# A hybrid diffusion backbone on one core: expert outputs of units 0 to 4 written as gated rows to DRAM, and another order of vector work at the dense mixer's start

## The reference

```python
def swiglu(x, wg, wu, wd):
    return (jax.nn.silu(x @ wg) * (x @ wu)) @ wd      # hidden width 2816

def moe_swiglu(x, w_router, wg, wu, wd):
    xt = x.reshape(-1, d)                              # 256 tokens
    logits = (xt @ w_router).astype(jnp.float32)
    top_v, top_i = lax.top_k(logits, TOP_K)            # 2 of 8
    top_w = jax.nn.softmax(top_v, axis=-1)
    gate = jnp.sum(jax.nn.one_hot(top_i, N_EXPERTS) * top_w[..., None], axis=1)
    out = jnp.zeros_like(xt)
    for e in range(N_EXPERTS):
        out = out + gate[:, e:e + 1] * swiglu(xt, wg[e], wu[e], wd[e])
    return out.reshape(bsz, t_len, d)
```

## Time and profile before

| | us |
|---|---|
| median of three runs (1506.99 to 1511.18) | 1510.18 |
| the profiled execution | 1505.23 |
| its span, from first to last instruction | 1503.3 |
| TensorE busy in it | 1446.7 (96%) |
| VectorE / ScalarE busy | 539.9 / 305.0 |

### The profile page before, as it was taken

The page is one execution under the profiler, slowest core; times in us unless marked ns, Lnnn a source line. Parts: engine busy times, 40 slices in busy tenths (PEclk is TensorE's granted clock), DMA queues, the critical chain, the costliest instruction groups (busy, mean ns, idle before and its releaser), DMA issues.

```text
span 1503.3 us, 60959 instructions
## 1 busy us (share of the span) xinstructions
PE 1446.7 (96%) x27189; PEld 1279.1 (85%) x27189; DVE 539.9 (36%) x1480; ACT 305.0 (20%) x877; POOL 26.0 (2%) x48
## 2 busy tenths in 40 slices
PE   5999998999999999999999999999999999999997
PEld 3888587999547787888878989999999999999996
DVE  1474426666637354888722210010101010010102
ACT  2112423000103523455342010100101010010101
POOL 0100000000000000100000000000000000000000
PEclk9999999999999999999999999999999999999999
DMA  9823849444449132100155999999999999999995
GB/s 390 320 94 123 312 162 408 173 170 167 177 168 350 56 127 86 36 8 6 35 228 200 419 378 408 417 380 418 376 419 382 413 418 372 418 381 418 381 411 227
DMA packets 71418, 406.98 MB, mean 271 GB/s; under 512 B 8530, under 2 KB 8964, under 8 KB 34436
## 3 DMA queue, kind: packets, MB, share of 16 engines
q1 hardware_dynamic: 68752, 399.96, 67.2%
q0 software_dynamic: 1440, 2.89, 0.7%
q10 hardware_dynamic: 1108, 2.41, 0.4%
HBM read 403.31 MB, written 1.92 MB: 270 GB/s over the span
## 4 chain that ended last, share of the span: by engine, by line
PE 92%; DVE 3%; DMA 2%; ACT 2%; issue 1%; ACTq 0%; DVEq 0%
PE banks L1648 28%; PE banks L1668 14%; PE banks L1030 9%; PE banks L1067 4%; PE banks L678 3%; PE banks L681 3%; PE banks L784 3%; PE banks L787 3%; PE banks L1194 2%; PE banks L1253 2%; PE banks L1630 2%; PE banks L1614 1%; PE banks L1271 1%; PE banks L704 1%; PE banks L820 1%; PE banks L1282 1%
## 5 line engine op out<-in xcount | busy, mean ns | idle before, releaser
L1648 PE MATMUL banks<-w,ring 128*64 128x86 f32 x11264 | 455.6, 237 | 1.4 <-issue 0.9
L1648 PEld LDWEIGHTS banks<-w,ring 128*64 128x64 f32 x11264 | 435.5, 136 | 9.9 <-issue 9.1
L1668 PE MATMUL banks<-w,ring 128*64 128x86 f32 x5632 | 242.1, 238 | 0.0
L3134 DVE TENSOR_TENSOR w<-w,banks 128x86 f32<-128x86 f32 x176 | 43.1, 245 | 551.7 <-PE banks L1648 544.0
L1668 PEld LDWEIGHTS banks<-w,ring 128*64 128x64 f32 x5632 | 224.1, 137 | 0.2 <-issue 0.2
L2193 ACT ACTIVATE w<-banks 128x86 f32<-128x86 f32 x176 | 42.7, 243 | 573.2 <-PE banks L1648 573.2
L704 PE MATMUL banks<-ring,ct 128*32 128x256 f32 x768 | 47.6, 396 | 2.3 <-ACT ct L1759 2.1
L678 PE MATMUL banks<-w,ring 128*128 128x256 f32 x224 | 49.2, 380 | 0.6 <-issue 0.3
L681 PE MATMUL banks<-ring,w 128*128 128x256 f32 x224 | 48.9, 379 | 0.0
L678 PEld LDWEIGHTS banks<-w,ring 128*128 128x128 f32 x224 | 42.3, 190 | 7.4 <-issue 1.8
L1030 PE MATMUL banks<-ht,ring 128*128 128x128 f32 x352 | 44.6, 282 | 3.0 <-DVE ht L2262 3.0
(11 more groups left out here) (466 smaller groups left out, 1757.6 us busy)
## 6 DMA issues: line engine op xcount, KB each, us to landing
ring<-in_moe_gu SPq DMA_DIRECT2D x176, 1024.0 KB, 8.7
ring<-in_moe_w_down SPq DMA_DIRECT2D x176, 512.0 KB, 8.8
ring<-in_ada_w SPq DMA_DIRECT2D x48, 1024.0 KB, 5.1
ring<-in_ev_w_in SPq DMA_DIRECT2D x11, 1024.0 KB, 26.3
ring<-in_ffn_w_gate SPq DMA_DIRECT2D x11, 1024.0 KB, 9.2
ring<-in_ffn_w_up SPq DMA_DIRECT2D x11, 1024.0 KB, 6.2
ring<-in_ffn_w_down SPq DMA_DIRECT2D x11, 1024.0 KB, 6.4
ring<-in_ev_w_out SPq DMA_DIRECT2D x4, 1024.0 KB, 6.4
```

The source lines that it names most:

```text
L1648: ins = [mm(b[hp, 0:CAP], w[:, k, hp], XG[:, k, :], start=k == 0, stop=k == KC - 1, skip_group_check=True) for hp in HALVES]
L1668: ins = [mm(bank[4 + c // 4][hp, (c % 4) * CAP:(c % 4 + 1) * CAP], w[:, c * P + hp.start:c * P + hp.stop], HIDU[:, t % 2, :], start=t == 0 ...
L3134: v.tensor_tensor(HIDU[:, t % 2, :], SILU[:, t % 2, :], bank[2 + t % 2][:, 0:CAP], ALU.mult).then_inc(sem("hid"), 1)
```

## The change

*Expert stage.* Five units (0 to 4) hand over their outputs in another way. The four scatter products and VectorE's four accumulations that stood in the unit behind them go. ScalarE copies the transposed outputs with a scale per row, the slot's gate, so that YG holds gated rows. GpSimd then writes the 86 rows with one indirect DMA to a DRAM buffer `sums`. Its row number for each slot is the token, plus 256 if the token is there by its second expert; empty slots go to rows of their own behind these. A token is in at most two experts, so each row is written at most once. TensorE makes the numbers and gates: two small products of SEL with a token table (`slots`) in place of the two transposes, and VectorE makes integers of them (`slot_rows`, behind strip 11). GpSimd fills the 512 rows with zeros before the stage, and reads them back in two loads, in units 6 and 7; VectorE adds both to O behind strip 11 of unit 7. Units 5 to 7 scatter by products as before. Unit 5, which needs the new border ahead and the old one behind, is now written out apart between two loops.

*Dense mixer.* On VectorE `modulated` and three of four input sums stand ahead of the first weight sums; TensorE's second product waits for three input sums and its fifth for the fourth.

The diff, cut to its core:

```diff
@@ -165,6 +168,8 @@
+  c[:, C_TOK:C_TOK + NST] = row + P * np.arange(NST)[None, :]
+  c[:, C_BASE:C_BASE + 2] = (2 * NST * P + row) * np.array([[1, -1]])
@@ -644,9 +660,22 @@
+      for n in range(2):
+        load(SUMS[n * NST * P:(n + 1) * NST * P, :], t["zeros"][0].partition_broadcast(NST * P), "rows_written")
+      with pool.Fori(1, ROW_UNITS + 1) as u:
+        pool.wait_ge(sem("unit_yg"), u * 2)
+        pool.wait_ge(sem("rows_written"), u * 16 + 16)
+        pool.sem_inc(sem("settled"), 1)
+        pool.indirect_dma_start(SUMS[:, :], bass.IndirectOffsetOnAxis(ap=SLOT_ROW[0:CAP, 0:1], axis=0),
+                    YG[0:CAP, :], None).then_inc(sem("rows_written"), 16)
+      pool.wait_ge(sem("rows_written"), rows_written(ROW_UNITS))
+      for n in range(2):
+        pool.wait_ge(sem("unit_yg"), 2 * (NE - 2 + n))
+        load(W[8 + n][:, :].rearrange("p (s n) -> p s n", s=NST),
+           SUMS[n * NST * P:(n + 1) * NST * P, :].rearrange("(s p) n -> p s n", p=P), "rows_written")
@@ -1038,7 +1067,7 @@
-          pe.wait_ge(sem("x_sums"), 4)
+          pe.wait_ge(sem("x_sums"), 3)
@@ -1049,6 +1078,8 @@
+          if j == 0:
+            pe.wait_ge(sem("x_sums"), 4)
@@ -1630,14 +1661,21 @@
+      def slots(b, sel, tokens):
+        for st in range(NST):
+          ins = mm(b[0:CAP, 0:3], sel[:, st, :], tokens[:, st, :], start=st == 0, stop=st == 1)
+        ins.then_inc(sem("selt_done"), 1)
       pe.wait_ge(sem("sel"), 1)
-      gather()
+      gather(SEL0)
       due0 = list(walk.due)
-      def unit(u, prev=None):
-        later = not isinstance(u, int)
+      def unit(u, prev=None, rows=False, rows_before=False):
+        first_of_all = isinstance(u, int) and u == 0
+        scattered_before = not first_of_all and not rows_before
         def taken(ins):
           ins[0].then_inc(sem("tile_used0"), 1)
@@ -1686,37 +1724,50 @@
         pe.wait_ge(sem("xg"), u * 2 + 2)
         gate_up(0, once(moe_slot("gu", 0)), outputs_turned)
-        if later:
+        if scattered_before:
           pe.wait_ge(sem("unit_yg"), u * 2)
           scatter(0, 4, "scattered")
           scatter(1, 6, "scattered")
         gate_up(1, once(moe_slot("gu", 1)))
-        if later:
+        if scattered_before:
           pe.wait_ge(sem("unit_taken"), shifted_by(u, prev, 4, -2))
         down(0, f"slot{moe_slot('d', 0)}", once(moe_slot("d", 0)), u * HB + (FT + 1))
-        if later:
+        if scattered_before:
           pe.wait_ge(sem("unit_taken"), u * 4)
           pe.sem_inc(sem("settled"), 1)
-        for st in range(NST):
-          ins = tr(bank[6][0:CAP, st * P:(st + 1) * P], SEL[:, st, :], ident)
-        ins.then_inc(sem("selt_done"), 1)
+        if rows_before:
+          pe.wait_ge(sem("unit_yg"), u * 2)
+          pe.sem_inc(sem("scattered"), 4)
+        if not rows:
+          for st in range(NST):
+            ins = tr(bank[6][0:CAP, st * P:(st + 1) * P], SEL[:, st, :], ident)
+          ins.then_inc(sem("selt_done"), 1)
+        elif not first_of_all:
+          slots(bank[6], SEL, TOKENS)
...
-        pe.wait_ge(sem("selt"), u + 1)
+        if not first_of_all:
+          pe.wait_ge(sem("selt"), u + 1)
         if prev is None:
           pe.wait_ge(sem("sel"), u + 2)
-          gather()
+          if first_of_all:
+            slots(bank[0], SEL0, TOKENS0)
+          gather(SEL)
         down(HB - 1, "slot_last", u * 16 + 16, u * HB + (FT + HB))
-      unit(0)
+      unit(0, rows=True)
+      pe.wait_ge(sem("selt"), 1)
+      with pe.Fori(1, ROW_UNITS) as u:
+        unit(u, rows=True, rows_before=True)
+      unit(ROW_UNITS, rows_before=True)
-      with pe.Fori(1, last) as u:
+      with pe.Fori(ROW_UNITS + 1, last) as u:
@@ -2193,12 +2244,16 @@
-        for h in range(0 if isinstance(u, int) else 2):
+        for h in range(0 if isinstance(u, int) and u == 0 else 2):
           act.wait_ge(sem("y_turned"), shifted_by(u, prev, 2, h - 1))
-          A(YG[0:CAP, h * 512:(h + 1) * 512], bank[6 + h][0:CAP, :], ACT.Copy).then_inc(sem("unit_yg"), 1)
+          if h == 0:
+            act.wait_ge(sem("rows_written"), u * 16 + 16 if rows_before else rows_written(ROW_UNITS))
+          A(YG[0:CAP, h * 512:(h + 1) * 512], bank[6 + h][0:CAP, :], ACT.Copy,
+            scale=SLOT_GATE if rows_before else 1.0).then_inc(sem("unit_yg"), 1)
         silu(1, u * UT + (N_MOE + gate_taken(1)), u * HB + FT)
-        act.wait_ge(sem("selt_done"), u + 1)
-        A(SELT[:, :, :].rearrange("p s n -> p (s n)"), bank[6][0:CAP, 0:TW], ACT.Copy).then_inc(sem("selt"), 1)
+        if not rows:
+          act.wait_ge(sem("selt_done"), u + 1)
+          A(SELT[:, :, :].rearrange("p s n -> p (s n)"), bank[6][0:CAP, 0:TW], ACT.Copy).then_inc(sem("selt"), 1)
@@ -2566,8 +2624,6 @@
-      up_sums(0, 0)
-      up_sums(0, 1)
       modulated(2, 2, 1)
@@ -2577,9 +2633,11 @@
       v.tensor_tensor(xs(1), x(1, 1), xs(0), ALU.subtract).then_inc(sem("x_sums"), 1)
-      up_sums(0, 2)
+      up_sums(0, 0)
+      up_sums(0, 1)
       dve.wait_ge(sem("x_sums"), 3)
       v.tensor_tensor(xs(3), x(1, 0), xs(1), ALU.subtract).then_inc(sem("x_sums"), 1)
+      up_sums(0, 2)
       up_sums(0, 3)
       for n in (5, 6):
         mods(n)
@@ -3134,14 +3206,32 @@
+      def slot_rows(u, b):
+        dve.wait_ge(sem("selt_done"), u + 1)
+        if not isinstance(u, int):
+          dve.wait_ge(sem("rows_written"), rows_written(u))
+        v.tensor_scalar(SLOT_AT, b[0:CAP, 1:2], CST[0:CAP, C_BASE + 1:C_BASE + 2], CST[0:CAP, C_BASE:C_BASE + 1],
+                ALU.mult, ALU.add).then_inc(made("dve_chain"), 1)
+        dve.wait_ge(sem("dve_chain"), so_far("dve_chain"))
+        v.tensor_tensor(SLOT_AT, SLOT_AT, b[0:CAP, 0:1], ALU.add).then_inc(made("dve_chain"), 1)
+        dve.wait_ge(sem("dve_chain"), so_far("dve_chain"))
+        v.tensor_copy(SLOT_ROW[0:CAP, :], SLOT_AT).then_inc(made("dve_chain"), 1)
+        dve.wait_ge(sem("dve_chain"), so_far("dve_chain"))
+        v.tensor_copy(SLOT_GATE, b[0:CAP, 2:3]).then_inc(sem("selt"), 1)
@@ -3166,33 +3254,53 @@
-        for st, h in ((0, 0), (0, 1), (1, 0), (1, 1)):
-          dve.wait_ge(sem("scattered"), shifted_by(u, prev, 4, 2 * st + h - 3))
-          o = O[:, st, h * 512:(h + 1) * 512]
-          v.scalar_tensor_tensor(o, bank[4 + 2 * st + h][:, :], GT1[:, st:st + 1], o,
-                       ALU.mult, ALU.add).then_inc(made("unit_taken"), 1)
-          dve.wait_ge(sem("unit_taken"), so_far("unit_taken"))
-        v.tensor_copy(GT1, GTU[:, :, bass.ds(u, 1)].rearrange("p s a -> p (s a)")).then_inc(made("unit_chain"), 1)
-        dve.wait_ge(sem("unit_chain"), so_far("unit_chain"))
+        if not rows_before:
+          for st, h in ((0, 0), (0, 1), (1, 0), (1, 1)):
+            dve.wait_ge(sem("scattered"), shifted_by(u, prev, 4, 2 * st + h - 3))
+            o = O[:, st, h * 512:(h + 1) * 512]
+            v.scalar_tensor_tensor(o, bank[4 + 2 * st + h][:, :], GT1[:, st:st + 1], o,
+                         ALU.mult, ALU.add).then_inc(made("unit_taken"), 1)
+            dve.wait_ge(sem("unit_taken"), so_far("unit_taken"))
+        else:
+          for _ in range(4):
+            dve.sem_inc(made("unit_taken"), 1)
+        if not rows:
+          at = slice(u, u + 1) if isinstance(u, int) else bass.ds(u, 1)
+          v.tensor_copy(GT1, GTU[:, :, at].rearrange("p s a -> p (s a)")).then_inc(made("dve_chain"), 1)
+          dve.wait_ge(sem("dve_chain"), so_far("dve_chain"))
         mixed(1, u * HB + (FT + 2), u * UT + (N_MOE + up_taken(1)))
         if prev is None:
-          next_selection(u)
+          next_selection(u, rows)
         for t in range(2, HB):
           mixed(t, u * HB + (FT + t + 1), u * UT + (N_MOE + up_taken(t)))
-      per = {"unit_chain": 3, "sel": 1, "unit_taken": 4}
+          if t == HB // 2 and rows:
+            slot_rows(u, bank[6])
+          if t == HB // 2 and prev is not None:
+            dve.wait_ge(sem("rows_written"), rows_written(ROW_UNITS) + 32)
+            for n in range(2):
+              v.tensor_tensor(Of, Of, W[8 + n][:, :], ALU.add).then_inc(made("dve_chain"), 1)
+              dve.wait_ge(sem("dve_chain"), so_far("dve_chain"))
```

More of the change, by code:

```diff
@@ L44 @@
 UNITS = NE + 5
+ROW_UNITS = 5
 HB = 22
@@ L1677, in outputs_turned @@
                 def outputs_turned():
-                    if not later:
+                    if first_of_all:
                         return
@@ L2211, in unit @@
                       ACT.Copy).then_inc(sem("xg"), 1)
-            unit(0)
+            unit(0, rows=True)
+            with act.Fori(1, ROW_UNITS) as u:
+                unit(u, rows=True, rows_before=True)
+            unit(ROW_UNITS, rows_before=True)
             act.wait_ge(sem("table"), 1)
@@ L2216, in _ @@
             prev = act.value_load(TBL[0:1, UNITS + 2:UNITS + 3], min_val=NE - 2, max_val=UNITS - 2)
-            with act.Fori(1, last) as u:
+            with act.Fori(ROW_UNITS + 1, last) as u:
                 unit(u)
@@ L3191, in _ @@
```

(13 more changed lines are left out.)

53 lines of the change are left out of this document (40 added, 13 removed).

## The result

The changed kernel takes 1501.12 us (median, 1498.74 to 1501.45), the kernel before 1509.66 in the same job: ratio 0.995, interval 0.9938 to 0.9962. The profiled execution took 1501.12 us, its span is 1498.8. The forecast, 1490, and its range, 1485 to 1500, were too low. The prediction had 1485.1 for the profiled execution and added 5.0 us, by which the runs before lay over theirs. Here the profiled execution is the median, so in it the forecast is 16 us off, and the added 5.0 hid a part of the error by luck.

What follows compares the result with a forecast made beforehand. Within a unit the DMA was taken as slower than TensorE, which lives on border lead. Expert stage 14.9 plus dense mixer 5.2 gave 20.1 us off 1505.2, so 1485.1; 5.0 carried over made 1490, range 1485 to 1500.

Steps and rivals of the forecast that it cites:

- What bounds the kernel: Expert stage: within a unit the DMA is slower than TensorE by 0.18 us a strip; TensorE lives on border lead.
- Rival A: Expert stage: TensorE's saving arrives whole, 23.1 us off, 1487; chance 0.14.
- Scatter products, slot products: Expert stage: scatter products removed in units 1 to 5 save 18.2 us; slot products added in units 0 to 4 cost 0.3.
- The row write: Starts of units 1 to 5: writing 86 rows, spread over sixteen engines, costs 1.1 us of DMA time each, 5.5 in all.
- Rival B: Row write: rows go over two engines, others each time; TensorE waits 4.9 us in unit 1; 1492; chance 0.16.
- One more hiccup as in unit 1: Expert stage: code of the unit written out apart raises TensorE's waits from 2 us to 3 us.
- Reading back: Units 6 and 7: each 1 MiB load takes 2.5 us of DMA, border lead 4.3 against a fall of 2.9; nothing waits.
- ACT and GpSimd waits: Expert stage: ScalarE's and VectorE's added waits for the row write cost 0, and would cost only beyond 40 us.
- C: Row write dear for all engines, some 2.6 us each: 11 us of waits, 12 won, 1498; chance 0.11.
- D: Row write: the same one or two engines take all rows each time; 33.5 us of waits, 10 slower, 1520; chance 0.05.
- E: Row write takes over 40 us to land and VectorE stops: slower; chance 0.02.
- Dense mixer: Dense mixer's start: first product at 239.0 without the clock's fall, second at 241.5 instead of 246.98; 5.2 us won.

Runs made afterwards that it cites:

- the second execution: The changed kernel run once more with nothing changed, beside the kernel before: 1501.44 us, ratio 0.9949.

## Why the prediction failed, step by step

*What bounds the kernel.* Right, and more so than I used it: the DMA's share of 1.02 and a lead of a few us decide. Rival A is out.

*Scatter products, slot products.* Right: with one row written, units 2 to 4 take 82.8 to 82.9 against 82.9 planned.

*The row write.* The first step that failed: "Nearest is the spread form; I take 1.1 us". The form is two engines; five writes took 7.8 us from the stage, where the balance of lead had 2.1 us of waits. Rival B had the mechanism, with 7.1 us for each of the two engines (the records have 0.159 us a packet, so 43 take 6.8). Its other half, that after unit 1 the remaining engines' lead covers the later pairs, fell short: units 2 to 4 lost 6.8 us (4.9 in the second execution), and the lead falls at the write in each unit. That the pair is another each time isn't shown.

*"One more hiccup as in unit 1, from the code of the unit that is now written out apart".* The second, and larger, step: I put 1 us on it. The hiccup of the kernel before, 0.85 us at unit 1's start, has no instruction packet near it (the last one started 60 us earlier); it is the wait at the table, which in the change only moved to unit 6. So I took the price of one kind of wait for another's. Written apart on the kernel before, the unit costs 3.7 to 4.3 us of the stage. In the change, TensorE has two such waits in unit 5 alone (timeline of both engines):

```profile
1232.33 0.24 DVE L3206 TENSOR_TENSOR w<-w,banks 128x86 f32<-128x86 f32 x1 [1.93 <-PE banks L1686]
...
1235.88 0.24 DVE L3206 TENSOR_TENSOR w<-w,banks 128x86 f32<-128x86 f32 x1 [3.30 <-PE banks L1686]
...
1236.58 1.41 PE L1706 MATMUL banks<-w,ring 128*64 128x86 f32 x32 [0.87 <-DVE w L3206]
...
1242.59 0.23 PE L1706 MATMUL banks<-w,ring 128*64 128x86 f32 x1 [1.03 <-issue]
```

The second stands in the middle of one run of 32 down products, whose tile had landed: no data was missing. The first is put down to VectorE, but wrongly: a down product needs `mixed` of the strip before, and that was done at 1232.57, four microseconds earlier (the one at 1235.88 is the next strip's). It is of the same kind: it ends 2.4 us behind the start of a packet of q8, and the second 2.3 us behind the next.

*Reading back, "nothing waits".* For the ring this was right: the border to unit 6 gave 6.7 us of lead at strip 5, more than the 4.3 forecast (two waits of TensorE just ahead of it, 1.7 us, helped), and 3.0 were left at strip 21. Even so the stage is 1.9 us shorter without the readbacks (3.6 against the second execution), by waits for code that went. The prediction had no term by which a transfer could cost beside new code.

The account, in us of the stage: forecast 671.5, measured 685.6, 14.1 over. The row writes took 7.8 instead of 2.1, so 5.7 of it. The other 9.3 are there with one row written too (677.8 against 686.4 - 17.9 = 668.5), where the forecast had 0.9: 8.4. In that kernel no gate/up tile from unit 1 on lands less than 1.7 us ahead of its use, so these loads hold nothing up. Its waits of TensorE in the stage (L1685 is gate and up, L1705 down, L3205 `mixed`):

```profile
PE banks L1705 <- issue: 4.2, 3, 2.4
PE banks L1685 <- issue: 3.4, 6, 1.3
PE banks L1705 <- DVE w L3205: 1.0, 1, 1.0
```

They make 8.6 us, 7.7 more than the 0.9 of the kernel before, and all but the 0.9 at the table end behind a packet of q8: most of the 9.3 is waiting for code. The split alone accounts for 3.7 to 4.3 of it, and some 1.9 go without the readbacks. Why the same number of packets costs 3 to 4 us more in the changed kernel than in the split one is open. The excess is largest in unit 5, over plan by 3.5 with one row written and by 4.5 without readbacks, by 1.1 to 1.4 where only the code was split.

*ACT and GpSimd waits.* Right: the write landed 16.6 to 21.7 us later, under the 40 us from which it would count. Rivals C (2.5 us for all five writes on sixteen engines, not 11), D (33.5 us of waits) and E are out. One engine is dear, as D has it: 1530 with 89 rows.

*Dense mixer.* Right: products at 238.85 and 241.48, forecast 239.0 and 241.5; 5.5 us there, against 5.2 taken. The last dense product came 5.4 us sooner. Not all of it reached unit 0, which started 3.7 sooner. At the last conditioning product ahead of the router 4.9 us were left (777.04 against 781.96). From there to unit 0 it took 22.45 us instead of 21.25. In the router TensorE's granted clock is 1.00 or 0.50, the lower level, and it falls at moments that differ between executions. After, it was at 0.50 from 791.6 on, behind 1.6 us in which TensorE had worked 0.23. In the kernel without readbacks it was at 1.00 up to 792.4, and in the 1.8 us to 789.8 TensorE had worked 1.0. The same window in the two:

```profile
793.00:796.00 3.00, 2.12 (x25) 2.02 (x26) 0.86 (x5) 0.00 (x0) 0.00 (x0) 0.50 0.00 0
```

```profile
793.00:796.00 3.00, 3.00 (x56) 3.00 (x58) 0.03 (x1) 0.46 (x1) 0.00 (x0) 0.65 0.03 5
```

In kernels with the same code up to there, unit 0 starts anywhere from 797.4 to 800.5: some 1.4 us of this come in the router, the others stand there before it. That is scatter of 3 us which one profile can't tell from an effect; the forecast carried none for it.

## What to carry to other kernels

Where the DMA runs at full share and TensorE lives on a lead, write down the lead at each border, and charge to it the engine time of every added transfer by the engines that it can use; make the row count a multiple of 16. Count what is written a second time: a unit peeled out of a loop has a price though it executes the same work, so carry one more table entry to keep one loop. And a plan with several small gains needs each part run alone: here one part was the whole of the result.
